# Feed-forward loop: VectorE makes the whole low part of each weight unit, GpSimd none, and VectorE's turn is reordered

## What is computed

```
h2 = rms_norm(x, g_pre_ffn) * (1 + scale2) + shift2
gt, up = split(h2 @ w_ffn_in)          # 1024 -> 2 x 2816
f = (silu(gt) * up) @ w_ffn_out        # 2816 -> 1024
x = x + gate2 * rms_norm(f, g_post_ffn)
# second block
mod = silu(c_2) @ w_ada_2 + b_ada_2    # 1024 -> 6 x 1024, for one vector
h = rmsnorm(x, norm1_g) * (1 + sc1) + sh1
proj = h @ w_in                        # q, k, v, u
...                                    # attention, pooling, residual
x = x + g2 * peer_ffn(h2)              # gathers 256 expert rows for each token
```

## Time and profile before

| | us |
|---|---|
| median of three runs | 1225.44 |
| lowest and highest | 1225.4, 1228.1 |
| the profiled execution | 1230.56 |
| its span in the profile | 1228.9 |
| TensorE busy | 1091.7 |
| VectorE busy | 861.7 |
| ScalarE busy | 496.2 |
| GpSimd busy | 436.9 |

### The profile page before, as it was taken

One profiled execution on the slowest core, in us unless ns is written; L12 is line 12 of the kernel. 1 busy time (PEld: TensorE's weight loads), 2 busy tenths in 40 slices (PEclk: granted clock), 3 DMA queues, 4 the chain that ended last, 5 costly groups with the idle time before them and its releaser, 6 DMA issues.

```text
span 1228.9 us, 13858 instructions
## 1 busy us (share of the span) xinstructions
PE 1091.7 (89%) x4690; PEld 721.7 (59%) x4690; DVE 861.7 (70%) x1761; ACT 496.2 (40%) x1135; POOL 436.9 (36%) x360
## 2 busy tenths in 40 slices
PE   3999999989999999998999999977877878778876
PEld 3899899878989988865656555423322333223222
DVE  5666458976888888727797848668568486685555
ACT  3226243263333336435534344433434334325344
POOL 0234222033333342303453545643433534344420
PEclk9999999999999999999999999998898989999999
DMA  9857666565787883655999999999999999999994
GB/s 379 329 201 278 254 260 225 220 240 206 284 303 295 311 314 125 245 208 209 422 407 423 421 421 420 422 422 421 422 421 421 421 421 421 421 421 422 421 422 180
DMA packets 57945, 414.08 MB, mean 337 GB/s; under 512 B 6432, under 2 KB 6432, under 8 KB 8352
## 3 DMA queue, kind: packets, MB, share of 16 engines
q0 software_dynamic: 41328, 296.24, 58.5%
q1 hardware_dynamic: 16416, 116.87, 24.9%
q10 hardware_dynamic: 144, 0.26, 0.1%
HBM read 412.30 MB, written 1.05 MB: 336 GB/s over the span
## 4 chain that ended last, share of the span: by engine, by line
PE 44%; DMA 30%; DVE 14%; ACT 6%; issue 5%; POOL 1%; SPq 0%; DVEq 0%; ACTq 0%; POOLq 0%
PE ps L1071 13%; DMA gate_area<-in_experts,idx 9%; DMA areas_seam<-in_experts,idx 6%; DMA spare<-in_experts,idx 6%; PE ps L489 5%; PE ps L502 4%; PE ps L504 4%; PE ps L503 4%; PE ps L543 4%; DVE mod_ring L1756 3%; DMA ring<-in_experts,idx 3%; DMA ring<-in_stream 3%; DMA ring<-in_experts,part_buf 2%; DVE w_lo L1762 2%; PE ps L998 1%
## 5 line engine op out<-in xcount | busy, mean ns | idle before, releaser
L1478 ACT ACTIVATE act<-now 128x1 f32<-128x1 f32 x256 | 50.8, 198 | 265.9 <-DVE now L2327 263.5
L1071 PE MATMUL ps<-areaB,c_row 128*128 128x512 f32 x232 | 112.9, 617 | 23.4 <-ACT c_row L1486 23.2
L1756 DVE CUSTOM_DVE_ANT_0 mod_ring<-mod_ring,c_row 128x1024 f32<-128x1024 f32 x84 | 112.1, 1387 | 16.8 <-DMA mod_ring<-in_mod_w 16.6
L1486 ACT ACTIVATE c_row<-small,act 128x128 f32<-128x128 f32 x256 | 102.8, 402 | 16.3 <-PE ps L1071 0.4
L1632 POOL DMA_INDIRECT areaB<-in_experts,idx x58 | 66.1, 1139 | 119.4 <-PE ps L1071 59.9
L1575 POOL TENSOR_TENSOR w_lo<-ring,w_hi 128x512 fp32r<-128x512 f32 x41 | 77.9, 1910 | 84.8 <-ACT w_hi L1213 84.7
L1071 PE MATMUL ps<-ring,c_row 128*128 128x512 f32 x192 | 94.6, 625 | 15.0 <-ACT c_row L1486 14.3
L502 PE MATMUL ps<-hT_h,w_lo 128*128 128x256 f32 x352 | 99.1, 282 | 0.8 <-DVE hid_l L2023 0.8
L503 PE MATMUL ps<-hT_l,w_hi 128*128 128x256 f32 x352 | 98.9, 281 | 0.0
L504 PE MATMUL ps<-hT_h,w_hi 128*128 128x256 f32 x352 | 98.8, 281 | 0.0
L1213 ACT ACTIVATE w_hi<-ring 128x2048 fp32r<-128x2048 f32 x41 | 78.4, 1913 | 47.8 <-PE ps L504 41.0
(11 more groups left out here) (444 smaller groups left out, 2574.5 us busy)
## 6 DMA issues: line engine op xcount, KB each, us to landing
ring<-in_stream SPq DMA_DIRECT2D x75, 1024.0 KB, 5.2
mod_ring<-in_mod_w POOLq DMA_DIRECT2D x24, 1024.0 KB, 5.2
mod_ring<-in_mod_w SPq DMA_DIRECT2D x18, 1024.0 KB, 7.3
gate_area<-in_mod_w SPq DMA_DIRECT2D x3, 1024.0 KB, 14.8
areaB<-in_mod_w SPq DMA_DIRECT2D x3, 1024.0 KB, 24.7
gate_area<-in_stream SPq DMA_DIRECT2D x3, 1024.0 KB, 13.0
small<-in_small SPq DMA_DIRECT2D x1, 1352.0 KB, 28.0
c_row<-in_c_rows SPq DMA_DIRECT2D x2, 512.0 KB, 15.8
```

Source lines behind the costliest of these rows:

```text
L1071: last = mm(ps[:, B3 + 2 * b + t, :], spread_w[n // FEW % 2][:, n % FEW, :], row[ROW_OF[n]][:, D + 512 * b:D + 512 * b + 512], start=first ...
L1486: A(spread_w[n // FEW % 2][:, n % FEW, :], c_("ident"), ACT.Identity, scale=weight)\
L1756: V.tensor_tensor_reduce(w, w, silu, 1.0, 0.0, ALU.mult, ALU.add, column).then_inc(mod_summed, 1)
```

## The change

For the units from gu 4 to qk2 1 (SHARED0 to SHARED1) VectorE makes the whole low part of 2048 columns, and GpSimd makes none; for the units ahead and behind, the parts stay as they were. SHARED(u) says which units are made by both engines, and POOL_PARTS(u) counts GpSimd's parts up to a unit. TensorE and SP wait for lo_pool for the shared units alone. SP's loop of loads is cut in three pieces, so that the loads in the middle have no such wait. VectorE's turn is in another order: the down unit's low part behind hidden(0), then the two dot products of the first modulation unit, hidden(1), the other two with the sum, and the odd gate-up's low part. In the turn behind the loop the order stays and the parts are whole.

```diff
--- before.py
+++ after.py
@@ -62,6 +62,7 @@
 SPLIT0 = AT["gu", 0]
 SPLITS = AT["wo2", 1] - SPLIT0
 HALF = 3 * UNIT // 4
+SHARED0, SHARED1 = SPLIT0 + 5, AT["qk2", 2]
 FRONT0, FRONT1 = AT["sc", 1], AT["gl", 11] + 1
 FRONTS = FRONT1 - FRONT0
 
@@ -72,6 +73,16 @@
 MOD_SP = 24
 MODS_BEHIND_LOAD = {2: 8, AT["sc", 1] + RING: 10, AT["qk", 1] + RING: 12, AT["z", 1] + RING: 14,
                     AT["gl", 1] + RING: 16, AT["gl", 2] + RING: 18, AT["gl", 4] + RING: 20, AT["gl", 6] + RING: 22}
+
+
+def SHARED(u):
+
+    return u < SHARED0 or u >= SHARED1
+
+
+def POOL_PARTS(u):
+
+    return sum(SHARED(v) for v in range(SPLIT0, u + 1))
 
 
 def DONE(kind, j):
@@ -410,11 +421,12 @@
             sp.dma_start(sm[:, n_late:], small[:, n_late:]).then_inc(late_in, 16)
             sp.dma_start(c_row[:, D:2 * D], c_rows[:, D:2 * D]).then_inc(c2_in, 16)
 
-            def load(i, s, split):
+            def load(i, s, split, shared=False):
 
                 if split:
                     sp.wait_ge(lo_dve, RING * i + (s - RING + 1 - SPLIT0))
-                    sp.wait_ge(lo_pool, RING * i + (s - RING + 1 - SPLIT0))
+                    if shared:
+                        sp.wait_ge(lo_pool, POOL_PARTS(RING * (i - 1) + s))
                 else:
                     sp.wait_ge(unit_done, RING * i + (s - RING + 1))
                 sp.dma_start(slot[s], stream[bass.ds(RING * i + s, 1)].rearrange("o p n -> p (o n)"))\
@@ -434,11 +446,16 @@
                 for s in range(RING):
                     load(i, s, False)
                     front_mods(RING * i + s)
-            for s in range(RING):
-                load(edge, s, RING * edge + s >= SPLIT0 + RING)
-            with sp.Fori(edge + 1, edge2) as i:
+            alone0, alone1 = -(-(SHARED0 + RING) // RING), (SHARED1 + RING) // RING
+            for i in range(edge, alone0):
+                for s in range(RING):
+                    load(i, s, RING * i + s >= SPLIT0 + RING, SHARED(RING * (i - 1) + s))
+            with sp.Fori(alone0, alone1) as i:
                 for s in range(RING):
                     load(i, s, True)
+            for i in range(alone1, edge2):
+                for s in range(RING):
+                    load(i, s, True, SHARED(RING * (i - 1) + s))
             assert RING * edge2 == SPLIT0 + SPLITS + RING
 
             def load_query(h):
@@ -494,7 +511,8 @@
 
                 u = AT[kind, j]
                 pe.wait_ge(lo_dve, u - SPLIT0 + 1)
-                pe.wait_ge(lo_pool, u - SPLIT0 + 1)
+                if SHARED(u):
+                    pe.wait_ge(lo_pool, POOL_PARTS(u))
                 return w_hi[u % RING], w_lo[u % RING]
 
             def mm3(o, lhs, rhs, start, stop, **kw):
@@ -869,7 +887,6 @@
                 def parts_of(n):
                     u0 = AT["gu", 4] + n
                     pe.wait_ge(lo_dve, 3 * i + (u0 - SPLIT0 + 1 - 6))
-                    pe.wait_ge(lo_pool, 3 * i + (u0 - SPLIT0 + 1 - 6))
                     return w_hi[u0 % RING], w_lo[u0 % RING]
 
                 w = parts_of(0)
@@ -1568,10 +1585,10 @@
                 pool.dma_start(cut(mod_ring, (m % 2) * UNIT, UNIT),
                                mod_w[bass.ds(i * 2 + m, 1)].rearrange("o p n -> p (o n)")).then_inc(mod_in[m % 2], 16)
 
-            def split_lo(u, i=0):
+            def split_lo(u):
 
                 s = u % RING
-                pool.wait_ge(hi_ready, i * RING + (u - SPLIT0 + 1))
+                pool.wait_ge(hi_ready, u - SPLIT0 + 1)
                 nc.gpsimd.tensor_tensor(w_lo[s][:, HALF:], slot[s][:, HALF:], w_hi[s][:, HALF:].bitcast(F32),
                                         ALU.subtract).then_inc(lo_pool, 1)
 
@@ -1590,17 +1607,11 @@
             split_lo(SPLIT0 + 3)
             split_lo(SPLIT0 + 4)
             with pool.Fori(1, PAIRS - 1) as i:
-                split_lo(SPLIT0 + 5 - 3, i)
                 load_mod(28, i)
                 load_mod(29, i)
-                split_lo(SPLIT0 + 6 - 3, i)
-                split_lo(SPLIT0 + 7 - 3, i)
             pool.dma_start(cut(areaA, 4096, 2048), band).then_inc(band_in, 16)
-            split_lo(AT["dn", PAIRS - 1])
-            split_lo(AT["qk2", 0])
             pool.wait_ge(mod_summed, 2 * (MODS - 1))
             pool.dma_start(query_w[0], stream[AT["wq", 0]]).then_inc(query_arrived(0)[0], 16)
-            split_lo(AT["qk2", 1])
             hT_split(2)
             for u in range(AT["qk2", 2], SPLIT0 + SPLITS):
                 split_lo(u)
@@ -1755,12 +1766,18 @@
                 silu = c_row[:, D * (m // 24):D * (m // 24) + D]
                 V.tensor_tensor_reduce(w, w, silu, 1.0, 0.0, ALU.mult, ALU.add, column).then_inc(mod_summed, 1)
 
-            def split_lo(u, i=0):
+            def split_lo(u):
+
+                s = u % RING
+                dve.wait_ge(hi_ready, u - SPLIT0 + 1)
+                V.tensor_tensor(w_lo[s][:, 0:HALF], slot[s][:, 0:HALF], w_hi[s][:, 0:HALF].bitcast(F32),
+                                ALU.subtract).then_inc(lo_dve, 1)
+
+            def split_lo_whole(u, i):
 
                 s = u % RING
                 dve.wait_ge(hi_ready, i * RING + (u - SPLIT0 + 1))
-                V.tensor_tensor(w_lo[s][:, 0:HALF], slot[s][:, 0:HALF], w_hi[s][:, 0:HALF].bitcast(F32),
-                                ALU.subtract).then_inc(lo_dve, 1)
+                V.tensor_tensor(w_lo[s], slot[s], w_hi[s].bitcast(F32), ALU.subtract).then_inc(lo_dve, 1)
 
             def mod_unit(m):
 
@@ -2034,31 +2051,34 @@
             split_lo(SPLIT0 + 4)
             dve.sem_inc(mod_step, 1)
             with dve.Fori(1, 1 + MOD_TURNS) as i:
-                split_lo(SPLIT0 + 5 - 3, i)
+                split_lo_whole(SPLIT0 + 5 - 3, i)
                 dve.wait_ge(unit_done, 3 * i + (AT["dn", 0] - 3 + 1))
                 hidden(0, i)
-
-                dve.wait_ge(mod_step, i)
-                for n in range(2):
+                split_lo_whole(SPLIT0 + 6 - 3, i)
+
+                def turn_dots(n):
                     dve.wait_ge(mod_in[n], 16 * i + (mod_arrived(26)[1]))
                     for b in range(2):
                         mod_dot(26 + n, b, turn_sums[:, 2 * n + b:2 * n + b + 1])
+
+                dve.wait_ge(mod_step, i)
+                turn_dots(0)
+                hidden(1, i)
+                turn_dots(1)
                 dve.wait_ge(mod_summed, 4 * i + 2 * MOD_FRONT)
                 V.tensor_tensor(modT[:, bass.ds(4 * i + (2 * MOD_FRONT - 4), 4)], turn_sums,
                                 c_("mod_b")[:, bass.ds(4 * i + (2 * MOD_FRONT - 4), 4)], ALU.add).then_inc(mod_step, 1)
-                hidden(1, i)
-                split_lo(SPLIT0 + 6 - 3, i)
-                split_lo(SPLIT0 + 7 - 3, i)
-
-            split_lo(SPLIT0 + 5 - 3, PAIRS - 1)
+                split_lo_whole(SPLIT0 + 7 - 3, i)
+
+            split_lo_whole(SPLIT0 + 5 - 3, PAIRS - 1)
             dve.wait_ge(unit_done, 3 * (PAIRS - 1) + (AT["dn", 0] - 3 + 1))
             hidden(0, PAIRS - 1)
             mod_unit(MODS - 2)
             dve.wait_ge(*mod_arrived(MODS - 1))
             mod_dot(MODS - 1, 0, mod_columns(MODS - 1)[0])
             hidden(1, PAIRS - 1)
-            split_lo(SPLIT0 + 6 - 3, PAIRS - 1)
-            split_lo(SPLIT0 + 7 - 3, PAIRS - 1)
+            split_lo_whole(SPLIT0 + 6 - 3, PAIRS - 1)
+            split_lo_whole(SPLIT0 + 7 - 3, PAIRS - 1)
             modulation(24, MOD_FRONT)
             step(V.scalar_tensor_tensor(out=cols[:, 32:40], in0=modT[:, 56:64], scalar=1.0, in1=c_("norm1"),
                                         op0=ALU.add, op1=ALU.mult))
```

## The result

Twenty runs of each kernel: 1222.78 us after (1218.88 to 1226.19) and 1228.51 before (1225.04 to 1230.96). The ratio is 0.995 with a 95% interval of 0.994 to 0.996, so the change takes 0.5% off: by the ratio 6.1 us (4.9 to 7.4), by the two medians 5.7. In two later sessions the ratio was 0.9949 (0.9933 to 0.9966) and 0.9945 (0.9924 to 0.9966). The forecast was 6.9 us and 1218.6 us. The gain lies where it was forecast; the time lies above the range, 1216.5 to 1221.8.

The account below looks back on a forecast made before the run. TensorE was taken to bound the kernel, with a stall ahead of each down unit in the feed-forward loop. Nine turns of 0.76 us gave 6.9 us off and the exit 0.0: 1225.44 - 6.9 = 1218.6 us, range 1216.5 to 1221.8.

Parts of the forecast that it names:

- The stall and its size: Ahead of the down unit in the nine loop turns: TensorE stalls 0.76 us a turn, 16.84 us without it.
- the refill: At a down unit's start: its first matmul takes 0.34 us to the next start against 0.23, 0.11 more.
- 4.6 us of recorded idle: In the loop: TensorE's nine recorded waits for VectorE's low part, 4.6 us in all, said to understate the stall.
- Its cause: In the loop: GpSimd's splits clash with VectorE's hidden(1) subtraction, 3.18 us, making the down unit's low part late.
- The parts' price and the schedule: VectorE's loop turn: a whole split takes 2.28 us, 2.20 start to start; the down split and hidden(1) have 3.6 to spare.
- D: As a time: start of the first matmul behind a down unit; as a rival: VectorE becomes the bound, slower, chance 0.06.
- Exit: Behind the loop, last hidden(1) to modulation: two whole splits, 4.40 us where it was 4.44, so 0.0 change.
- B: Rival: part of the gain comes back, by a shorter stall or 1 to 3 us at the exit; chance 0.12.
- C: Rival: no change, 1225.4 us, since the gap ahead of the down unit is TensorE's own; chance 0.06.
- the step from the gain to a time: Whole kernel: the profiled 1230.56 us lies 5.1 above the median 1225.44; 6.9 off that median gives 1218.6.

Follow-up runs that it names:

- the clash with no use: Changed kernel with VectorE's old order, plus two unused GpSimd subtractions of 512 columns each turn: 1226.10 us, ratio to the kernel before 0.9984.
- the run with the entry's edit: Changed kernel with VectorE making the whole low parts of down unit 0 and gate-up 3 earlier, GpSimd none: 1221.46 us, changed kernel 1220.71.
- the kernel with the useless work and the new order: Changed kernel plus two unused GpSimd subtractions in each turn behind the second load issue: 1221.15 us, ratio 0.9929.

## Why the prediction was off, point by point

**The stall and its size: right.** It rested on starts, not on the recorded idle: 0.76 us a turn, 16.84 without it; measured 16.84 to 16.85 in eight turns and 16.90 in the first. Over the nine turns 158.43 - 151.67 = 6.76 us, and 0.11 more at the exit, where the refill of the last of the nine down units is counted: 6.87, forecast 6.9. The 4.6 us of recorded idle would have been 2.3 short. The timed runs agree: 6.1 us (4.9 to 7.4).

**Its cause: right, and shown** by the clash with no use. The Trainium skill's rule of the exclusive lock ("SBUF — State Buffer", section "SBUF: two separate sides") holds in so far as one engine blocks fully; that whoever starts first wins doesn't fit here either: in the run with the useless pair VectorE's subtraction is recorded at 338.41, GpSimd's pair at 338.63, and VectorE waits for both. This rests on recorded starts, which the profile gives only roughly for GpSimd, so which engine was really first is open.

**The parts' price and the schedule: right.** Forecast 2.28 us and 2.20 start to start, measured 2.292 and 2.21. Down split at D + 2.2 to 4.4: 328.49 to 330.78 with D at 326.3. The odd gate-up's split from D + 10.5: 336.76. Exit 4.40: 4.41.

**Rivals.** B, C and D fall: nothing of the gain was given back, the gap was no property of TensorE's own, and the turn stayed bound by TensorE.

**What failed is the step from the gain to a time:** "It lies 5.1 above the median of the runs, 1225.44, so against the median: 1225.44 - 6.9 = 1218.6". The term that failed is 1225.44, the level of the kernel before, taken from three runs with no width of its own. Twenty runs put it at 1228.51, 3.1 us higher; that is 3.1 of the 4.2 us between 1218.6 and the measured 1222.78. The other 1.1 us lies between the forecast gain of 6.9 and the 5.7 of the two medians, and inside the interval of 4.9 to 7.4. The medians of the kernel before in four sessions were 1228.51, 1228.43, 1229.65 and 1227.48, over runs from 1224.99 to 1234.04; on the first of them the forecast is 1228.51 - 6.9 = 1221.6, and, since single runs lie up to some 3 us to either side of a median and three of them can all lie on one side, it needs a range of that size for the level alone. The profiled execution, 1230.56, was set aside for the median of three; it was high but not odd, since four of the twenty runs were above it. The range held only the unknowns of the change.

Where does the spread of the level come from? Windows of the profiles before, after, and of the run with the entry's edit (the columns are those of the earlier trace rows):

```profile
55.00:60.00 5.00, 5.00 (x37) 4.87 (x36) 5.00 (x8) 1.54 (x2) 2.72 (x2) 0.86 0.60 190
60.00:65.00 5.00, 5.00 (x14) 4.01 (x15) 4.93 (x13) 0.00 (x0) 0.31 (x1) 0.50 0.06 23
65.00:70.00 5.00, 5.00 (x34) 4.72 (x33) 3.05 (x6) 0.66 (x2) 0.00 (x0) 0.96 0.00 0
...
270.00:275.00 5.00, 4.35 (x25) 4.35 (x26) 4.69 (x11) 3.55 (x4) 4.30 (x5) 0.66 0.61 211
```

```profile
55.00:60.00 5.00, 5.00 (x40) 4.82 (x40) 5.00 (x9) 1.54 (x2) 2.29 (x2) 1.00 0.55 193
60.00:65.00 5.00, 5.00 (x19) 4.13 (x18) 4.93 (x13) 0.00 (x0) 0.28 (x1) 0.66 0.06 20
65.00:70.00 5.00, 5.00 (x35) 4.71 (x34) 3.01 (x6) 1.54 (x2) 0.70 (x1) 1.00 0.23 80
...
270.00:275.00 5.00, 5.00 (x45) 5.00 (x44) 4.49 (x8) 1.99 (x2) 2.75 (x3) 1.00 0.46 188
```

```profile
60.00:65.00 5.00, 5.00 (x33) 4.64 (x32) 4.97 (x12) 0.00 (x0) 0.71 (x1) 1.00 0.03 11
```

TensorE's granted clock falls to 1.2 GHz at about 58 and 270 us in some executions and not in others. A window of 5 us at 0.66 has (1 - 0.66) x 5 / 0.5 = 3.4 us at the lower level; such 3.4 us are called a dip here, and 6.8 us in one piece are two. Counted so over the stretch from 20 us to the loop, the profiles with one such dip start down unit 0 at 286.98 to 287.10, with two at 288.22 to 288.51, with three at 289.98 to 290.14, with four at 291.33: 1.3 to 1.7 us a dip between the middles of these groups. The profiles with the entry's edit, none at 284.58, one at 286.30 and three at 289.21, fit once its 0.85 is added. Between the profiles before and after, 2.9 us of the 10.3 are two such dips, and no effect of the change on them is shown: the changed kernel has one or two, the kernel before has three both times, and the kernel with the useless work and the new order has three as well. Some 0.6 us more lie in the stage "norm", by one dip there. The last stage moves too, from 661.9 to 664.4 us over all profiles, without regard to the change. What makes a dip come in one execution and not in the next is open; I made no run for it. The traces do show one thing that goes with it, at a time when all these kernels still do the same work: the trace's first record of the full clock begins at 20.7 to 21.3 us in the profiles with three or four dips, at 22.0 to 22.4 with one, at 22.6 to 23.1 with two and at 23.35 with none. Whether the runs of the kernel before near 1225.4 us are those with fewer dips is not shown: both its profiles have three.

## What to carry to other kernels

Measure a stall from start to start of the stalled engine's instructions and multiply by its turns; then ask what is late, not who is busy: here the late part came ahead of its due time either when GpSimd's share was gone or when both engines made theirs earlier, and doing both adds nothing. Moving it in one engine's queue alone cost some 9 us, because the other engine's part became the late one. When two engines lock each other out, it costs only where the loser's result is due, so move the due work ahead of the clash or the clash away from it. And give the level of the kernel before a width of its own, since a gain of 0.5% is smaller than the spread of its runs.

## What the runs showed that I had not expected

- A GpSimd subtraction of 512 columns with one tensor as both inputs takes 1.02 us (2.04 for two), and with two tensors about 1.28 (2.55 for two). The output's type differs as well (fp32 and fp32r), so that no run shows which of the two makes the difference.
- GpSimd's load issues take 0.53 to 0.57 us in the profiles whatever VectorE runs beside them, two-input instructions too (317.00 to 317.53 us in the changed kernel, beside a subtraction and a dot product).
- The nine turns repeat to 0.03 us between the profiled executions of a kernel, while the timed ones spread by 6 us and more: in the profiles the spread lies in the other stages, ahead of the loop above all.
